# Query and key rows cross DRAM once in float32, and GpSimd splits them per head

## The chip, the cores and the metric

One core of a Trainium2 chip runs the whole kernel. The metric is the device time of one execution in microseconds, the median of several runs. One core has TensorE (matrix products into PSUM), VectorE, ScalarE, GpSimd and SyncE (SP, which here issues all DMAs, in order, on one queue).

## The reference

Two sequences of 1024 tokens (width 1024, float32) go through one encoder layer with shared weights:

- `h = rmsnorm(x)`, then one input projection into q, k, v of mixer A (8 heads x 64) and the compressed c_q (256), c_kv (128), k_rope (32) of mixer B.
- Mixer A: rotary on q and k, then attention with three (window, dilation) patterns merged by their softmax denominators. The kernel computes it as one dense softmax with a table of log counts (`logc`) added to the scores.
- Mixer B: q = rmsnorm(c_q) @ w_uq (64 + 32 rotary columns a head), k and v from rmsnorm(c_kv) @ w_ukv, a rotary key that the heads share, dense softmax.
- Both outputs are normalised, concatenated and projected by w_o, with a residual; then a gated MLP (2816 wide) with a width-3 convolution over positions, residual, final rmsnorm.

## The kernel before, in words

**Precision.** Products are made of float32r matmuls on pairs: each float32 operand is split into a high part (a copy to float32r, on ScalarE) and a low part (the operand less the high part, on VectorE), and a product takes three passes hi*hi, hi*lo, lo*hi. All engines run their own instruction stream; semaphores (`s_...`) tie them together. The work of each engine stands in program order, so an instruction that waits holds up what stands behind it, and so does a DMA issue that waits on SP.

**Stages, for each of the two sequences:**

1. *Query and key products of mixer A* (`qk_unit`, U = 0..3, token half h = 0, 1, so r = 2U + h = 0..7; each U needs two weight tiles w_hi/w_lo, split by `w_hi_split` on ScalarE and `w_lo_split` on VectorE). VectorE rotates the product (`rope`, L1093) into `mc`, ScalarE makes `rq_hi` (`rope_hi`, L806), VectorE `rq_lo` (`rope_lo`, L1106), and SP writes both parts to DRAM (`write_qk`, L259, 8 DMAs for each r). Going through DRAM turns the layout into one of rows per head.
2. *v products* (16, L547 on; `v_hi` L819 on ScalarE, `v_lo` L1124 on VectorE), with weights `vst` loaded by `load_vc` (L268) and split by `vc_hi` (L811) and `vc_lo` (L1111). `load_vc(s, 2)` and `load_vc(s, 3)` bring the two halves of the weight w_c of the next stage. In ScalarE's and VectorE's order their splits stand behind v_hi/v_lo 9 and 11, ahead of 12 to 15.
3. *c products* (8 token tiles), normalised and transposed. The first waits for the whole split of w_c (s_vwl) and for v_lo(12).
4. *Attention A* (`attention`, PE at L564, ScalarE at L880, VectorE at L1212): 64 steps, 8 heads x 8 query tiles. A step G: scores(G+3), row_max and nm on VectorE, exp on ScalarE, transposes of the probabilities, their split pt_hi/pt_lo, and the products with v. scores takes the head's rows in `q2`, `khh`, `kll`, in two buffers, which `load_head_a` (L279, 5 DMAs, 1.5 MB) fills from DRAM for both parts; it waits for the scores of two heads earlier.
5. *Projections of mixer B* (14 units, i = 0..13: 0 and 1 rotary q, then q and k in turn to 9, then v in 10..13), in three PSUM pairs. For i < 10 ScalarE makes `b_hi`, VectorE `b_lo` (three buffers of each), SP writes both to DRAM (`write_b`, L304). Unit i from 5 on waits for b_lo of unit i - 3. The rotary key of all heads is transposed at i = 5 and placed in both heads' buffers (`krh`, `krl`).
6. *Attention B*: the same steps with three score passes; `load_head_b` (L291) brings 8 pieces for a head. Before it ScalarE and VectorE wait until every row of stage 5 has been written.
7. *Output projection, MLP*, with TensorE busy nearly throughout. `wo_split(0)` is hooked into attention B at step 40.

GpSimd only splits the weights of mixer B (uq, ukv) at the start of attention A.

**Memory.** The output of the attentions, `o` (32 KB a partition at R_O), lies where wv_hi/wv_lo, the v weights, were. `qh, ql, kh, kl` lie where `q2, khh, kll` and `logc` are.

**SP's order around the change** (L370 to L409): load_vc(2), write_qk(6), write_qk(7), load_head_a(0), logc, load_vc(3), a wait for the c products, load_head_a(1), the weights of mixer B, the other heads of A; then write_b(0) to write_b(3), the rotary key, load_head_b(0), load_head_b(1), write_b(4) to write_b(9), wost, gout, and the other heads of B.

## Time and profile before

| what | value |
|---|---|
| median of 3 runs | 3044.6 us (3040.99 to 3048.77) |
| the profiled execution | 3046.3 us, of which the span of the trace 3044.5 us |
| TensorE (PE) busy | 2922.4 us, 96% |
| VectorE (DVE) busy | 1788.0 us, 59% |
| ScalarE (ACT) busy | 1228.1 us, 40% |
| GpSimd (POOL) busy | 16.8 us, 1% |
| mean granted clock of TensorE | 0.982 |
| DMA | 227.5 MB, mean 75 GB/s |

The table says that TensorE is the engine to look at, and that VectorE and ScalarE have time to spare on average. An average says nothing of a stage: to judge a change, one looks for the stretches in which TensorE stands, and for what released it. A line number in a row is that of the instruction; L467 (`product`) and L1072 (`sub`) are helpers that many stages use, so their rows are told apart by the tiles named. The number in brackets at the end of a row of the timeline is how long the engine had been idle and which instruction released it.

### The profile page before, as it was taken

To read this page: it belongs to the slowest core of one execution; us is meant where nothing else is said; L and a number is where in the kernel's file an instruction comes from. 1 tells how busy PE (TensorE), PEld (TensorE's weight loads), DVE (VectorE), ACT (ScalarE), POOL (GpSimd) and SP (SyncE) were. 2 spreads that over 40 slices of the span, in tenths; PEclk is the share of its full clock that TensorE was granted. 3 is DMA by queue.
4 is the path that set the end of the run, shared out by engine and by line. 5 is a ranking of instruction groups with operands and counts; after the bars stand their busy time and mean duration, and the time that the engine had idled before them with its cause. 6 is when DMAs were issued, how large, how long until landed. Compare 5 with 4: busy or idle time off the path is not lost.

```text
span 3044.5 us, 39362 instructions
## 1 busy us (share of the span) xinstructions
PE 2922.4 (96%) x16272; PEld 2550.9 (84%) x16272; DVE 1788.0 (59%) x2559; ACT 1228.1 (40%) x1990; POOL 16.8 (1%) x12
## 2 busy tenths in 40 slices
...
GB/s 222 149 61 87 43 170 86 80 45 75 31 56 50 76 56 49 56 49 57 61 191 125 59 77 43 200 72 65 46 70 35 49 56 49 42 49 49 49 49 56
DMA packets 170177, 227.50 MB, mean 75 GB/s; under 512 B 23440, under 2 KB 122640, under 8 KB 169488
## 3 DMA queue, kind: packets, MB, share of 16 engines
...
q14 instruction: 47, 0.39, 0.0%
...
## 4 chain that ended last, share of the span: by engine, by line
PE 89%; DVE 5%; ACT 2%; DMA 2%; issue 1%; SPq 1%; DVEq 0%; ACTq 0%
PE pair L467 71%; PE pair L606 7%; PE pair L582 4%; PE pair L583 4%; PE pair L591 2%; DMA q_nope_rows<-b_lo 1%; DVE at_lo L1072 1%; DMA xs<-in_x_t 1%; PE pair L472 0%; DMA xt<-in_x_seqs 0%; ACT at_hi L947 0%; ACT junk L766 0%; DVE at_lo L1082 0%; DVE b_lo L1072 0%; DVE x L1068 0%
## 5 line engine op out<-in xcount | busy, mean ns | idle before, releaser
L467 PE MATMUL pair<-at_hi,wu_hi 128*128 128x512 f32 x1408 | 549.3, 390 | 5.2 <-DVE at_lo L1072 5.2
L467 PE MATMUL pair<-at_hi,wu_lo 128*128 128x512 f32 x1408 | 549.1, 390 | 0.0
L467 PE MATMUL pair<-at_lo,wu_hi 128*128 128x512 f32 x1408 | 549.1, 390 | 0.0
L1072 DVE TENSOR_TENSOR pt_lo<-pair,pt_hi 128x512 fp32r<-128x512 f32 x512 | 329.9, 686 | 99.4 <-ACT pt_hi L902 99.4
L902 ACT CAST pt_hi<-pair 128x512 fp32r<-128x512 f32 x512 | 275.7, 590 | 162.5 <-PE pair L606 155.0
L1403 DVE TENSOR_TENSOR x<-pair,x 128x1024 f32<-128x1024 f32 x176 | 215.2, 1223 | 181.5 <-PE pair L467 180.9
L467 PEld LDWEIGHTS pair<-at_hi,wu_hi 128*128 128x128 f32 x1408 | 265.2, 188 | 60.7 <-DVE at_lo L1072 5.7
L467 PEld LDWEIGHTS pair<-at_hi,wu_lo 128*128 128x128 f32 x1408 | 265.0, 188 | 55.4
L467 PEld LDWEIGHTS pair<-at_lo,wu_hi 128*128 128x128 f32 x1408 | 265.0, 188 | 54.9
L887 ACT ACTIVATE prob<-pair,nm 128x1024 f32<-128x1024 f32 x256 | 289.4, 1131 | 14.6 <-DVE nm L1225 14.3
L467 PE MATMUL pair<-wd_hi,h_hi 128*128 128x512 f32 x704 | 275.4, 391 | 8.1 <-DVE x L1403 8.1
L582 PE MATMUL pair<-pt_hi,v 128*128 128x256 f32 x1024 | 268.6, 295 | 7.2 <-ACT ot L892 5.9
L467 PE MATMUL pair<-wd_lo,h_hi 128*128 128x512 f32 x704 | 275.0, 391 | 0.0
L467 PE MATMUL pair<-wd_hi,h_lo 128*128 128x512 f32 x704 | 274.9, 390 | 0.0
L606 PE MATMUL pair<-idn,prob 128*128 128x128 f32 x2048 | 268.3, 274 | 2.4 <-DVE pt_lo L1072 2.0
L583 PE MATMUL pair<-pt_lo,v 128*128 128x256 f32 x1024 | 257.6, 284 | 0.0
L1367 DVE SCALAR_TENSOR_TENSOR cv<-pair,cw,cv 128x1023 f32<-128x1023 f32 x42 | 53.9, 1282 | 316.0 <-ACT cv L990 316.0
L606 PEld LDWEIGHTS pair<-idn,prob 128*128 128x128 f32 x2048 | 230.8, 141 | 8.1 <-issue 6.1
L582 PEld LDWEIGHTS pair<-pt_hi,v 128*128 128x128 f32 x1024 | 195.8, 191 | 12.9 <-issue 6.3
L583 PEld LDWEIGHTS pair<-pt_lo,v 128*128 128x128 f32 x1024 | 196.7, 192 | 5.2
L960 ACT CAST wd_hi<-ust 128x1024 fp32r<-128x1024 f32 x44 | 44.3, 1052 | 345.0 <-PE pair L467 336.6
L990 ACT ACTIVATE cv<-pair,cw 128x1024 f32<-128x1024 f32 x42 | 50.7, 1207 | 296.8 <-PE pair L467 296.8
...
## 6 DMA issues: line engine op xcount, KB each, us to landing
ust<-in_w_up SPq DMA_DIRECT2D x88, 512.0 KB, 3.9
ust<-in_w_down SPq DMA_DIRECT2D x44, 512.0 KB, 4.4
wst<-in_w_qk SPq DMA_DIRECT2D x16, 512.0 KB, 4.8
...
xt<-in_x_seqs SPq DMA_DIRECT2D x16, 512.0 KB, 3.6
q<-q_rows SPq DMA_DIRECT2D x16, 512.0 KB, 3.6
...
```

The source lines that it names most:

```text
L467: mm = pe.matmul(dst, lhs, rhs, start=(i == 0), stop=(i == n - 1))
L582: pe.matmul(bank(6)[:, 0:2 * P], v2[:, k, h, :], pt_hi[g % 2][:, k, :], start=(k == 0), stop=False)
L583: mm = pe.matmul(bank(6)[:, 0:2 * P], v2[:, k, h, :], pt_lo[g % 2][:, k, :], start=False, stop=(k == NT - 1))
L591: mm = pe.matmul(bank(7)[:, i * HA:(i + 1) * HA], ot[:, i * P:(i + 1) * P], stk[:], start=True, stop=True)
L606: tr = pe.transpose(bank(4 + hb)[:, k * P:(k + 1) * P], prob[G % 2][:, c:c + P], idn[:])
L887: act.activation(prob[G % 2][:], pair[G % 2][:], ACT.Exp, bias=nm[:, G % 4:G % 4 + 1], scale=scale, accum_out=den[:, h % 2, t:t + 1]).then ...
L902: act.copy(pt_hi[G // 2 % 2][:, 4 * hb:4 * hb + 4, G % 2 * P:(G % 2 + 1) * P], bank(4 + hb).rearrange("p (k n) -> p k n", k=4)).then_inc(s ...
L960: act.copy(dst, ust[slot][:]).then_inc(s_uhi, 1)
L990: act.activation(dst[:], pair[b % 2][:], ACT.Identity, bias=cw[b][:, 3:4], scale=cw[b][:, 1:2]).then_inc(s_ci, 1)
L1072: return dve.tensor_tensor(out_, full, hi.bitcast(F32), ALU.subtract)
L1367: dve.scalar_tensor_tensor(buf[:, 1:S], u[:, 0:S - 1], cw[b][:, 0:1], buf[:, 1:S], ALU.mult, ALU.add).then_inc(s_c0, 1)
L1403: dve.tensor_tensor(x1[:, t, :], pair[2 + t % 2][:], x1[:, t, :], ALU.add).then_inc(s_ya, 1)
```

## The change

Rotated q and k (both mixers) are no longer split before they go to DRAM: one float32 row goes out and comes back. GpSimd then makes the high and low parts for each head, in the same two buffers per head as before (`head` in the gpsimd block, a single raw buffer for each of q and k). In mixer A the raw rows land in unused columns of `o`, so their first load waits for the end of the v products; in mixer B they land in R_REST, so that `wost` is loaded after the last split and its split moves from step 40 to 56. Mixer B's projections are evicted by one ScalarE copy each (`bst`, four buffers). Declarations, semaphore names and casts that only follow from this are left out; "..." marks what is left out.

```diff
--- before.py
+++ after.py
-B_WRITES = (4, 3, 3)
+B_WRITES = (3, 3, 2, 2)
...
-mcb = place("mcb", [P, 2, H], F32, R_X)
 msb = place("msb", [P, 2, H], F32, R_X + 4)
-b_hi = [place(f"b_hi{i}", [P, 2, H], F32R, R_X + 8 + 8 * i) for i in range(3)]
-b_lo = [place(f"b_lo{i}", [P, 2, H], F32R, R_X + 12 + 8 * i) for i in range(3)]
-krh = place("krh", [ROT, S], F32R, R_C + 25)
-krl = place("krl", [ROT, S], F32R, R_X + 60)
+bst = [place(f"bst{i}", [P, 2, H], F32, R_X + 8 + 4 * i) for i in range(4)]
+krt = place("krt", [ROT, S], F32, R_C + 25)
+
+
+qraw_a, kraw_a = o[:, 6:8, WA:D], o[:, 4:6, WA:D]
+qraw_b, kraw_b = place("qraw_b", [P, S], F32, R_REST), place("kraw_b", [P, S], F32, R_REST + 4)
...
     def write_qk(s, r):
         U, h = r // 2, r % 2
         dst, a = (kd if U % 2 == 0 else qd), U // 2
-        sp.wait_ge(s_rlo, 8 * s + r + 1)
-        for hl, src in ((0, rq_hi[r % 2]), (1, rq_lo[r % 2])):
-            for i in range(4):
-                to = dst[4 * a + i, hl].rearrange("(o f) s -> f o s", o=2)[:, :, half(h)]
-                sp.dma_start(to, src[ROT * i:ROT * i + ROT, :, :].bitcast(F32)).then_inc(s_qw[r % 2], 16)
+        sp.wait_ge(s_ro, 8 * s + r + 1)
+        for i in range(4):
+            to = dst[4 * a + i].rearrange("(o f) s -> f o s", o=2)[:, :, half(h)]
+            sp.dma_start(to, rq[r % 2][ROT * i:ROT * i + ROT, :, :]).then_inc(s_qw[r % 2], 16)
...
     def load_head_a(s, h):
-        e, a = h % 2, h // 4
-        if h >= 2:
-            sp.wait_ge(s_sc, 128 * s + 8 * (h - 2) + 8)
+        if h:
+            sp.wait_ge(s_hs, 16 * s + h)
         for i in range(2):
-            sp.wait_ge(s_qw[i], 512 * s + 256 * (a + 1))
-        sp.dma_start(q2[e][:], qd[h].rearrange("l f s -> (l f) s")).then_inc(s_hd[e], 16)
+            sp.wait_ge(s_qw[i], 256 * s + 128 * (h // 4 + 1))
         for j in range(2):
             rows = slice(HA * j, HA * j + HA)
-            sp.dma_start(khh[e][rows, :], kd[h, 0]).then_inc(s_hd[e], 16)
-            sp.dma_start(kll[e][rows, :], kd[h, 1]).then_inc(s_hd[e], 16)
+            sp.dma_start(qraw_a[rows, :, :], qd[h].rearrange("d (a n) -> d a n", a=2)).then_inc(s_hd, 16)
+            sp.dma_start(kraw_a[rows, :, :], kd[h].rearrange("d (a n) -> d a n", a=2)).then_inc(s_hd, 16)
 
     def load_head_b(s, h):
-        e, last = h % 2, 3 + 2 * (h // 2)
-        if h >= 2:
-            sp.wait_ge(s_sc, 128 * s + 64 + 8 * (h - 2) + 8)
-        for m in range(3):
-            sp.wait_ge(s_bwr[m], 32 * (B_WRITES[m] * s + len([i for i in range(last + 1) if i % 3 == m])))
-        for hl, qdst, kdst in ((0, qh, kh), (1, ql, kl)):
-            sp.dma_start(qdst[e][0:HA, :], qnd[hl, h * HA:(h + 1) * HA, :]).then_inc(s_hd[e], 16)
-            for o_ in range(2):
-                sp.dma_start(qdst[e][HA + 16 * o_:HA + 16 * o_ + 16, :],
-                             qrd[hl, o_, 16 * h:16 * h + 16, :]).then_inc(s_hd[e], 16)
-            sp.dma_start(kdst[e][0:HA, :], knd[hl, h * HA:(h + 1) * HA, :]).then_inc(s_hd[e], 16)
+        last = 3 + 2 * (h // 2)
+        if h:
+            sp.wait_ge(s_hs, 16 * s + 8 + h)
+        for m in range(4):
+            sp.wait_ge(s_bwr[m], 16 * (B_WRITES[m] * s + len([i for i in range(last + 1) if i % 4 == m])))
+        rows = slice(h * HA, (h + 1) * HA)
+        sp.dma_start(qraw_b[0:HA, :], qnd[rows, :]).then_inc(s_hd, 16)
+        for o_ in range(2):
+            sp.dma_start(qraw_b[HA + 16 * o_:HA + 16 * o_ + 16, :], qrd[o_, 16 * h:16 * h + 16, :]).then_inc(s_hd, 16)
+        sp.dma_start(kraw_b[0:HA, :], knd[rows, :]).then_inc(s_hd, 16)
 
     def write_b(s, i):
-        sp.wait_ge(s_bl, 14 * s + i + 1)
-        for hl, src in ((0, b_hi[i % 3]), (1, b_lo[i % 3])):
-            if i < 2:
-                to = qrd[hl].rearrange("o p s -> p o s")[:, :, half(i)]
-                sp.dma_start(to, src[:].bitcast(F32)).then_inc(s_bwr[i % 3], 16)
-            else:
-                dst, n = (qnd if i % 2 == 0 else knd), (i - 2) // 2
-                sp.dma_start(dst[hl, n * P:(n + 1) * P, :],
-                             src[:].bitcast(F32).rearrange("p a n -> p (a n)")).then_inc(s_bwr[i % 3], 16)
+        if i < 2:
+            sp.wait_ge(s_bro, 2 * s + i + 1)
+            to = qrd.rearrange("o p s -> p o s")[:, :, half(i)]
+            sp.dma_start(to, bst[i % 4][:]).then_inc(s_bwr[i % 4], 16)
+        else:
+            sp.wait_ge(s_bcp, 8 * s + i - 1)
+            dst, n = (qnd if i % 2 == 0 else knd), (i - 2) // 2
+            sp.dma_start(dst[n * P:(n + 1) * P, :], bst[i % 4][:].rearrange("p a n -> p (a n)")).then_inc(s_bwr[i % 4], 16)
...
+        sp.dma_start(logc[:], log_count).then_inc(s_logc, 16)
+        sp.wait_ge(s_vm, 16 * (s + 1))
         load_head_a(s, 0)
-        sp.wait_ge(s_qw[1], 512 * s + 512)
-        sp.dma_start(logc[:], log_count).then_inc(s_logc, 16)
         load_vc(s, 3)
-        sp.wait_ge(s_cm, NT * (s + 1))
         load_head_a(s, 1)
         sp.wait_ge(s_vwl, 4 * s + 4)
+        sp.wait_ge(s_cm, NT * (s + 1))
         sp.dma_start(uq_st[:], w_uq).then_inc(s_bw, 16)
         sp.dma_start(ukv_st[:], w_ukv).then_inc(s_bw, 16)
 
@@ -393,23 +388,23 @@
 
         for i in range(4):
             write_b(s, i)
-        sp.wait_ge(s_krl, s + 1)
-        for e in range(2):
-            sp.dma_start(kh[e][HA:HB, :], krh[:].bitcast(F32)).then_inc(s_krw, 16)
-            sp.dma_start(kl[e][HA:HB, :], krl[:].bitcast(F32)).then_inc(s_krw, 16)
+        sp.wait_ge(s_bfree, 2 * (s + 1))
         load_head_b(s, 0)
+        write_b(s, 4)
+        sp.wait_ge(s_krh, s + 1)
+        sp.dma_start(kraw_b[HA:HB, :], krt[:]).then_inc(s_krw, 16)
+        for i in range(5, 10):
+            write_b(s, i)
+        sp.dma_start(gout[:], g_out.partition_broadcast(P)).then_inc(s_og, 16)
         load_head_b(s, 1)
-        for i in range(4, 10):
-            write_b(s, i)
-        sp.dma_start(wost[:], w_o_v[:, :, 0:COL]).then_inc(s_wost, 16)
-        sp.dma_start(gout[:], g_out.partition_broadcast(P)).then_inc(s_og, 16)
         sp.wait_ge(s_bm, 14 * s + 14)
-        sp.wait_ge(s_krw, 64 * (s + 1))
         for h in range(2, HEADS):
             load_head_b(s, h)
             for t in range(NT):
                 if t * 6 // NT + 2 == h:
                     sp.dma_start(x1[:, t, :], x_v[s * NT + t]).then_inc(s_x1[t], 16)
+        sp.wait_ge(s_hs, 16 * (s + 1))
+        sp.dma_start(wost[:], w_o_v[:, :, 0:COL]).then_inc(s_wost, 16)
...
             if 3 <= i < 5:
                 pe.wait_ge(s_bfree, 2 * s + i - 2)
-            if i >= 5:
-                pe.wait_ge(s_bl, 14 * s + i - 2)
+            elif 5 <= i < 13:
+                pe.wait_ge(s_bcp, 8 * s + i - 4)
+            elif i == 13:
+                pe.wait_ge(s_bl, 4 * s + 1)
...
                 if t == 0:
-                    pe.wait_ge(s_hd[h % 2], head_landed(h))
+                    pe.wait_ge(s_hs, (2 * s + mixer) * HEADS + h + 1)
...
-        w_hi_split(s, 2)
-        w_hi_split(s, 3)
-        for r in range(3):
-            rope_hi(r)
-        w_hi_split(s, 4)
-        w_hi_split(s, 5)
-        rope_hi(3)
+        for j in range(2, 6):
+            w_hi_split(s, j)
         vc_hi(0)
...
-        for i in range(14):
+        for i in range(2, 14):
+            act.wait_ge(s_bm, 14 * s + i + 1)
             if i < 10:
-                src = mcb[:] if i < 2 else pair[i % 3][:].rearrange("p (a n) -> p a n", a=2)
-                act.wait_ge(s_bro if i < 2 else s_bm, 2 * s + i + 1 if i < 2 else 14 * s + i + 1)
-                free(act, s_bwr[i % 3], 32 * (B_WRITES[i % 3] * s + i // 3))
-                act.copy(b_hi[i % 3][:], src).then_inc(s_bh, 1)
+                free(act, s_bwr[i % 4], 16 * (B_WRITES[i % 4] * s + i // 4))
+                act.copy(bst[i % 4][:], pair[i % 3][:].rearrange("p (a n) -> p a n", a=2)).then_inc(s_bcp, 1)
...
-        for m in range(3):
-            act.wait_ge(s_bwr[m], 32 * B_WRITES[m] * (s + 1))
-        attention(1, SCALE_B, {40: lambda: wo_split(0), 63: lambda: o_stats(0)})
+        for m in range(4):
+            act.wait_ge(s_bwr[m], 16 * B_WRITES[m] * (s + 1))
+        attention(1, SCALE_B, {56: lambda: wo_split(0), 63: lambda: o_stats(0)})
...
         def rope(r):
-            h = r % 2
+            h, q = r % 2, rq[r % 2]
             src = pair[r % 3][:].rearrange("p (o n) -> p o n", o=2)
             dve.wait_ge(s_mq, 16 * s + 2 * r + 2)
-            free(dve, s_rlo, 8 * s + r)
+            free(dve, s_ro, 8 * s + r)
+            free(dve, s_qw[r % 2], 256 * s + 64 * (r // 2))
             if r < 2:
                 dve.wait_ge(s_tabs, 2 * s + r + 1)
-            dve.tensor_tensor(mc[:], src, cost[:, half(h)].unsqueeze(1).to_broadcast([P, 2, H]), ALU.mult).then_inc(s_mc, 1)
+            dve.tensor_tensor(q[:], src, cost[:, half(h)].unsqueeze(1).to_broadcast([P, 2, H]), ALU.mult)
             dve.tensor_tensor(ms[:], src, sint[:, half(h)].unsqueeze(1).to_broadcast([P, 2, H]), ALU.mult).then_inc(s_ms, 1)
             dve.wait_ge(s_ms, 8 * s + r + 1)
-            dve.tensor_tensor(mc[:, 0, :], mc[:, 0, :], ms[:, 1, :], ALU.subtract)
-            dve.tensor_tensor(mc[:, 1, :], mc[:, 1, :], ms[:, 0, :], ALU.add).then_inc(s_ro, 1)
-
-        def rope_lo(r):
-            dve.wait_ge(s_rhi, 8 * s + r + 1)
-            free(dve, s_qw[r % 2], 512 * s + 128 * (r // 2))
-            sub(rq_lo[r % 2][:], mc[:], rq_hi[r % 2][:]).then_inc(s_rlo, 1)
+            dve.tensor_tensor(q[:, 0, :], q[:, 0, :], ms[:, 1, :], ALU.subtract)
+            dve.tensor_tensor(q[:, 1, :], q[:, 1, :], ms[:, 0, :], ALU.add).then_inc(s_ro, 1)
...
-        for i in range(14):
-            src = pair[i % 3][:].rearrange("p (a n) -> p a n", a=2)
-                dve.tensor_tensor(mcb[:], src, cosbt[:, half(i)].unsqueeze(1).to_broadcast([P, 2, H]), ALU.mult)
-                dve.tensor_tensor(msb[:], src, sinbt[:, half(i)].unsqueeze(1).to_broadcast([P, 2, H]), ALU.mult).then_inc(s_bfree, 1)
-                dve.wait_ge(s_bfree, 2 * s + i + 1)
-                dve.tensor_tensor(mcb[:, 0, :], mcb[:, 0, :], msb[:, 1, :], ALU.subtract)
-                dve.tensor_tensor(mcb[:, 1, :], mcb[:, 1, :], msb[:, 0, :], ALU.add).then_inc(s_bro, 1)
...
+        for i in range(2):
+            src, q = pair[i][:].rearrange("p (a n) -> p a n", a=2), bst[i]
+            dve.wait_ge(s_bm, 14 * s + i + 1)
+            free(dve, s_bwr[i], 16 * B_WRITES[i] * s)
+            if i:
+                dve.wait_ge(s_bro, 2 * s + i)
+            dve.tensor_tensor(q[:], src, cosbt[:, half(i)].unsqueeze(1).to_broadcast([P, 2, H]), ALU.mult)
+            dve.tensor_tensor(msb[:], src, sinbt[:, half(i)].unsqueeze(1).to_broadcast([P, 2, H]), ALU.mult).then_inc(s_bfree, 1)
+            dve.wait_ge(s_bfree, 2 * s + i + 1)
+            dve.tensor_tensor(q[:, 0, :], q[:, 0, :], msb[:, 1, :], ALU.subtract)
+            dve.tensor_tensor(q[:, 1, :], q[:, 1, :], msb[:, 0, :], ALU.add).then_inc(s_bro, 1)
+            if i == 0:
+                last_osum()
+        for i in range(10, 14):
+            t = 2 * (i - 10)
+            dve.wait_ge(s_bh, 4 * s + i - 9)
+            sub(v2[:, t:t + 2, :, HA:P], pair[i % 3][:].rearrange("p (t h x) -> p t h x", t=2, x=HA),
+                v2[:, t:t + 2, :, 0:HA]).then_inc(s_bl, 1)
...
     for s in range(N_SEQ):
+        def head(mixer, h, copies, rests):
+            n, e = (2 * s + mixer) * HEADS + h, h % 2
+            pool.wait_ge(s_hd, 64 * (n + 1))
+            if n:
+                pool.wait_ge(s_hs, n)
+            if h >= 2:
+                pool.wait_ge(s_sc, 8 * (n - 1))
+            for to, raw in copies(e):
+                pool.tensor_copy(to, raw).then_inc(s_hh, 1)
+            pool.wait_ge(s_hh, 3 * n + 2)
+            k_rest, q_rest = rests(e)
+            sub(*k_rest).then_inc(s_hh, 1)
+            pool.wait_ge(s_hh, 3 * n + 3)
+            sub(*q_rest).then_inc(s_hs, 1)
+
+        halves = lambda a: a.rearrange("p (a n) -> p a n", a=2)
+        hi_a = lambda e: ((halves(q2[e][:]), qraw_a), (halves(khh[e][:]), kraw_a))
+        lo_a = lambda e: ((halves(kll[e][:]), kraw_a, halves(khh[e][:])),
+                          (halves(q2[e][HA:P, :]), qraw_a[HA:P, :, :], halves(q2[e][HA:P, :])))
+        hi_b = lambda e: ((qh[e][0:HB, :], qraw_b[0:HB, :]), (kh[e][0:HB, :], kraw_b[0:HB, :]))
+        lo_b = lambda e: ((kl[e][0:HB, :], kraw_b[0:HB, :], kh[e][0:HB, :]),
+                          (ql[e][0:HB, :], qraw_b[0:HB, :], qh[e][0:HB, :]))
+
+        head(0, 0, hi_a, lo_a)
+        pool.wait_ge(s_cm, NT * (s + 1))
+        head(0, 1, hi_a, lo_a)
         pool.wait_ge(s_bw, 32 * (s + 1))
+        pool.wait_ge(s_hs, 16 * s + 2)
         pool.tensor_copy(uq_hi[:], uq_st[:]).then_inc(s_bhi, 1)
         pool.tensor_copy(ukv_hi[:], ukv_st[:]).then_inc(s_bhi, 1)
         pool.wait_ge(s_bhi, 2 * s + 1)
-        pool.tensor_tensor(uq_lo[:], uq_st[:], uq_hi[:].bitcast(F32), ALU.subtract).then_inc(s_blo, 1)
+        sub(uq_lo[:], uq_st[:], uq_hi[:]).then_inc(s_blo, 1)
         pool.wait_ge(s_bhi, 2 * s + 2)
-        pool.tensor_tensor(ukv_lo[:], ukv_st[:], ukv_hi[:].bitcast(F32), ALU.subtract).then_inc(s_blo, 1)
+        sub(ukv_lo[:], ukv_st[:], ukv_hi[:]).then_inc(s_blo, 1)
+        pool.wait_ge(s_blo, 2 * s + 2)
+        for h in range(2, HEADS):
+            head(0, h, hi_a, lo_a)
+        pool.wait_ge(s_krw, 16 * (s + 1))
+        pool.wait_ge(s_max, 128 * s + 64)
+        for h in range(HEADS):
+            head(1, h, hi_b, lo_b)
```

## Rows read from the trace of the kernel before

**Rows 1.** The page: busy time of each engine, and the chain that ended last.
```profile
PE 2922.4 (96%) x16272; PEld 2550.9 (84%) x16272; DVE 1788.0 (59%) x2559; ACT 1228.1 (40%) x1990; POOL 16.8 (1%) x12
...
PE 89%; DVE 5%; ACT 2%; DMA 2%; issue 1%; SPq 1%; DVEq 0%; ACTq 0%
```

**Rows 2.** TensorE's waits, whole run: us in total, times, the longest.
```profile
PE pair L467 <- DVE b_lo L1072: 43.5, 8, 19.3
...
PE pair L467 <- DVE w_lo L1072: 9.5, 4, 4.0
```

**Rows 3.** Stretches: length; busy us of PE, PEld, DVE, ACT, POOL; PEclk, DMA share, GB/s.
```profile
202.00:402.00 200.00, 194.84 (x1416) 181.11 (x1416) 180.12 (x393) 155.39 (x298) 8.31 (x4) 0.99 0.25 68
402.00:464.00 62.00, 36.02 (x145) 27.28 (x143) 27.59 (x27) 15.76 (x17) 0.00 (x0) 0.83 0.74 246
464.00:685.00 221.00, 217.19 (x1501) 199.99 (x1502) 173.89 (x316) 155.29 (x294) 0.00 (x0) 0.99 0.24 63
73.30:80.00 6.70, 6.70 (x23) 5.39 (x24) 5.55 (x6) 2.09 (x2) 0.00 (x0) 0.77 0.87 232
449.00:456.00 7.00, 6.91 (x18) 5.34 (x19) 3.96 (x5) 3.95 (x4) 0.00 (x0) 0.55 1.03 420
```

**Rows 4.** Timeline, mixer B's projections of both sequences: start, duration in us.
```profile
401.92 0.40 PE L467 MATMUL pair<-ct_hi,uq_hi 128*128 128x512 f32 x1
402.15 0.40 PE L467 MATMUL pair<-ct_hi,uq_lo 128*128 128x512 f32 x1
...
439.48 0.43 SPq L312 DMA_DIRECT2D q_nope_rows<-b_lo  x1
...
446.77 1.01 ACT L917 CAST b_hi<-pair 128x1024 fp32r<-128x1024 f32 x1 [19.23 <-DMA q_nope_rows<-b_lo]
...
449.10 0.79 PE L467 MATMUL pair<-ukv_hi,ct_hi 128*128 128x512 f32 x1 [18.39 <-DVE b_lo L1072]
...
460.12 0.47 PE L467 MATMUL pair<-kh,qh 96*128 96x512 f32 x1 [2.41 <-issue]
...
1914.78 0.40 PE L467 MATMUL pair<-ct_hi,uq_hi 128*128 128x512 f32 x1
...
1973.31 0.47 PE L467 MATMUL pair<-kh,qh 96*128 96x512 f32 x1 [2.41 <-issue]
```

**Rows 5.** Timeline, query and key products of sequence 0.
```profile
73.30 0.77 PE L467 MATMUL pair<-at_hi,w_hi 128*128 128x512 f32 x1 [3.97 <-DVE w_lo L1072]
...
70.79 1.23 DVE L1072 TENSOR_TENSOR rq_lo<-mc,rq_hi 128x1024 fp32r<-128x1024 f32 x1 [1.11 <-ACT rq_hi L809]
```

**Rows 6.** DMA issues, 398 to 470 us: KB each, median us to landing.
```profile
q_nope_rows<-b_hi SPq DMA_DIRECT2D x4, 512.0 KB, 5.5
```

**Rows 7.** Timeline from v to c products; last row: DMA issues, 202 to 216.
```profile
151.31 0.34 SPq L276 DMA_DIRECT2D vst<-in_w_c  x1
...
155.93 1.58 ACT L817 CAST wc_hi<-vst 128x1664 fp32r<-128x1664 f32 x1 [2.29 <-DMA vst<-in_w_c]
...
159.43 0.87 DVE L1127 SCALAR_TENSOR_TENSOR v<-pair,xrs,v 128x256 fp32r<-128x256 f32 x2
...
164.49 0.35 PE L467 MATMUL pair<-wc_hi,at_hi 128*128 128x416 f32 x1
...
205.11 0.60 SPq L289 DMA_DIRECT2D kll<-k_rows  x1
...
uq_st<-in_w_uq SPq DMA_DIRECT2D x1, 768.0 KB, 8.1
```

**Rows 8.** Groups: GpSimd's of the run; pt_lo of 215.0 to 223.4, of the run.
```profile
L1459 POOL TENSOR_TENSOR ukv_lo<-ukv_st,ukv_hi 128x1024 fp32r<-128x1024 f32 x2 | 4.8, 2404 | 0.0
...
L1455 POOL CAST ukv_hi<-ukv_st 128x1024 fp32r<-128x1024 f32 x2 | 2.1, 1045 | 0.0
...
L1072 DVE TENSOR_TENSOR pt_lo<-pair,pt_hi 128x512 fp32r<-128x512 f32 x6 | 3.8, 682 | 0.0
...
L1072 DVE TENSOR_TENSOR pt_lo<-pair,pt_hi 128x512 fp32r<-128x512 f32 x512 | 329.9, 686 | 99.4 <-ACT pt_hi L902 99.4
```

More of the change, by code:

```diff
@@ L85, in encoder_kernel @@
         sint = place("sint", [P, S], F32, R_Q + 36)
-        mc = place("mc", [P, 2, H], F32, R_Q + 40)
         ms = place("ms", [P, 2, H], F32, R_Q + 44)
-        rq_hi = [place(f"rq_hi{i}", [P, 2, H], F32R, R_Q + 48 + 8 * i) for i in range(2)]
-        rq_lo = [place(f"rq_lo{i}", [P, 2, H], F32R, R_Q + 52 + 8 * i) for i in range(2)]
+        rq = [place(f"rq{i}", [P, 2, H], F32, R_Q + 48 + 4 * i) for i in range(2)]
         wv_hi = [place(f"wv_hi{i}", [P, NK, COL], F32R, R_O + 16 * i) for i in range(2)]
@@ L189, in encoder_kernel @@
         s_logc = sem("log_count_landed")
-        s_hd = [sem(f"head_rows_landed{i}") for i in range(2)]
+        s_hd, s_hh, s_hs = sem("head_rows_landed"), sem("head_rows_hi"), sem("head_rows_split")
         s_sc, s_max, s_nm, s_pr = sem("scores_ready"), sem("row_max"), sem("minus_max_ready"), sem("probs_ready")
@@ L194, in encoder_kernel @@
         s_bw, s_bhi, s_blo, s_tabb = sem("b_weights_landed"), sem("b_weights_hi"), sem("b_weights_lo"), sem("b_tables_landed")
[L195 to L197 removed]
+        s_bm, s_bfree, s_bro, s_bcp = sem("b_product_ready"), sem("b_product_taken"), sem("b_rotated"), sem("b_copied")
+        s_bh, s_bl = sem("b_v_hi"), sem("b_v_lo")
+        s_bwr = [sem(f"b_rows_written{i}") for i in range(4)]
+        s_krt, s_krh, s_krw = sem("k_rope_transposed"), sem("k_rope_copied"), sem("k_rope_placed")
         s_ss, s_std, s_rs, s_xn = sem("squares_summed"), sem("rms_ready"), sem("rrms_ready"), sem("tile_normalised")
@@ L562, in _, with attention @@
                         c_transposed(t - 1)
-                def attention(mixer, score_passes, head_landed, between=None):
+                def attention(mixer, score_passes, between=None):
                     b, bg = (2 * s + mixer) * STEPS, (2 * s + mixer) * GROUPS
@@ L804, in _ @@
                 tb = 2 * NT * s
-                def rope_hi(r):
-                    act.wait_ge(s_ro, 8 * s + r + 1)
-                    free(act, s_qw[r % 2], 512 * s + 128 * (r // 2))
-                    act.copy(rq_hi[r % 2][:], mc[:]).then_inc(s_rhi, 1)
                 def vc_hi(i):
@@ L855, in _ @@
                 vc_hi(1)
-                rope_hi(6)
-                rope_hi(7)
                 for i in range(16):
```

85 lines of the change are left out of this document (26 added, 59 removed).

## The prediction

> **What bounds the kernel now.** I read the page first. TensorE is busy 96% of the span and holds 89% of the chain that ended last [rows 1]. So a part of VectorE's or ScalarE's work that goes is worth nothing by itself; only what TensorE waits for counts. The view of who waited for whom, for TensorE, names two places that this change touches: 43.5 us behind the low halves of mixer B's rows (b_lo), 19.3 us of it at once, and 9.5 us behind w_lo [rows 2]. The table by stage shows where that lies: in the 62 us of mixer B's projections TensorE is busy 36 us at a mean clock of 0.83, while both attentions run near 98% busy [rows 3].
>
> *Mixer B's projections.* The first product starts at 401.92, the first scores of mixer B at 460.12: 58.2 us; in sequence 1, 1914.78 to 1973.31, 58.5 us [rows 4]. ScalarE stands 19.2 us before a b_hi copy because its buffer is still being written out, and TensorE stands 18.4 us behind it [rows 4]. The write it waits for was issued only at 439.48: on SP's queue, in order, both heads' loads (L400, L401) stood ahead of it [rows 4]. After the pause TensorE ran at a clock of 0.55 for 7 us [rows 3], so 0.45 * 7 = 3.2 us of work are lost on top. That is the lower of its two levels (1.2 of 2.4 GHz) for most of the stretch, and what it did before was to stand still.
>
> *Query and key products.* At 73.30 TensorE has waited 3.97 us for w_lo of the third unit. In the code ScalarE splits that weight only behind rope_hi(2), VectorE behind rope_lo(2), which ran at 70.79 [rows 5]. The clock is 0.77 over the next 6.7 us [rows 3]: 1.5 us more.
>
> **The change, part by part.**
>
> (a) Query/key stage. Eight rope_hi and eight rope_lo per sequence go, and half of the write DMAs. ScalarE can split weight 4 when the first half of unit (1, 1) is done, some 5 us before TensorE needs it at 73.3 - 4.0 = 69.3. VectorE reached it after rope_lo(2), at 70.79 + 1.2 = 72.0; each rope_lo cost it 1.23 us and a wait of 1.11 [rows 5], and of the three before this point the first lies in idle time before the second unit's table. So it comes 2 * 2.3 us earlier, at 67.3, and the low half is there at 68.5. Weight 5 can be split from 69.3 on, is done by 71.6, and is wanted half a unit later, 24 matmuls at 0.23 us or 5.5 us after 69.3. The wait goes: 4.0 + 1.5 = 5.5 us per sequence, **11 us**. Bounds: 4 in all if one of the two stays, 11 if both go. I take 11, as both are the same wait (4 waits, longest 4.0, [rows 2]). What is late next there is nothing up to the v products.
>
> (b) Projection stage of B. TensorE's own work is 6 units of 12 matmuls and 8 of 6, at 0.227 us from one start to the next (two starts in [rows 4], 0.23, and the 24 of two units at 5.45 us): 27.3 us, with last_osum and krot's transposes 28.5. The way from the last product to the first scores was 2.4 us [rows 4] and stays (a copy and a subtraction). Now the remaining waits, walked through queue by queue. Unit 4 waits for the second msb product: 0.1. Row buffers: write 3 is issued at about 414 and lands at 418.5 (5.5 us for a q_nope write at its median, [rows 6]; 4.5 for one alone, my choice, since half the bytes are gone); load_head_b(0) waits on SP for exactly that, takes 2.2 us of issue, and holds write 4 behind it until 421, landed 425.5; copy 8 needs that buffer, so unit 11 waits 0.1 and the later copies run 1 us behind; unit 13 waits about 1 us for v_lo(10), the last v_lo ends 1 us later than before. Sum 28.5 + 2.4 + 1.8 = 32.7 us. GpSimd must have head 0 split by then: rows and rotary key landed at about 424, plus 6.9 us (below) is 431, and scores would start at 434.6. So 3.6 us of margin; past them each us costs one. Gain (58.2 - 32.7) + (58.5 - 32.7) = **51 us**. Bounds: no waits left, 30.9 us, gives 55; head 0 late by 7 us, a whole split, gives 37. I take 51, as the walk has the split ahead. ScalarE and VectorE both wait for all writes; the last (copy 9, about 428) lands by 433, before scores(0) is finished.
>
> (c) The second half of w_c. Today load_vc(3) is issued at 151.31 while v products run, the split is done and TensorE goes over to the c products at 164.49 with no idle time [rows 7]. The raw buffers of mixer A lie in o, which is wv_hi/wv_lo of the second half, so load_head_a(0) must now wait for all 16 v products (s_vm), and load_vc(3) stands behind it on SP. ScalarE's vc_hi(3) stands before v_hi(12) and the c products wait for it. So TensorE stands from 164.5 on: four DMA issues at 0.60 and a little each [rows 7], 2.5 us; then the landing. Alone it takes 4.6 us (151.31 to 155.93); the weight load issued behind a whole head of 1.5 MB took 8.1 [rows 7]; behind 1 MB, in proportion, 4.6 + 3.5 * 2/3 = 6.9, which I take. From the landing to the first low half that TensorE needs 155.93 to 159.43 + 0.5 = 4.0. Sum 13.4 us. The clock after it by the row after the 18.4 us pause: 3.2 us, at least the 1.5 seen after the 4 us pause. Together 16.6, twice: **33 us lost**. Bounds per sequence: 2.5 + 4.6 + 4.0 + 1.5 = 12.6 and 2.5 + 8.1 + 4.0 + 3.2 + 2.4 (one GpSimd instruction in VectorE's way) = 20.2.
>
> (d) GpSimd's splits. A copy of 1024 columns by the ukv_hi row 1.04 us, a subtraction by the ukv_lo row 2.40 [rows 8]: 2 * 1.04 + 2 * 2.40 = 6.9 us per head (the half of q2 has as many columns, so no less). A step of attention takes 200/64 = 3.1 us in A and 221/64 = 3.45 in B, a head 25 and 28. Load, 2.5 us of issue, 5 to 6 landing and the split fit twice. Head 1 of A starts on GpSimd when the c products end and is wanted some 20 us later; the weight splits of 8.3 us follow it and head 2 follows them, still about 15 us ahead. Head 1 of B: issued at 431 behind gout, landed 438, split 445, wanted some 24 us after the first scores. Nothing on the path while TensorE sets the pace. Is VectorE slowed by it? While GpSimd made its four weight splits (215.0 to 223.4), pt_lo took 682 ns, over the whole run 686 [rows 8]: no.
>
> (e) wost is loaded after the last split and split at step 56, not 40. GpSimd ends head 7 about two steps after step 45, the load of 1 MB lands some 9 us later, at step 50. The same two instructions, covered by the slack of 221 - 174 us that VectorE has in this stage [rows 3]; without that cover 1.9 us on ScalarE, twice. Cost nothing. Writes and reads of rows fall by half; no stage is bound by them but (b), where it is counted. The rest of the diff (types, names) costs nothing.
>
> **Sum:** -11 - 51 + 33 = -29 us against the profiled execution's own 3046.3 (span 3044.5 and 1.8 around it): 3017. The median of the runs shown is 1.7 us lower, so I say **3016**.
>
> **A rule against it.** VectorE's wc_lo reads two SBUF tiles, and no row of this trace shows such an instruction beside GpSimd. Head 0's rows are issued from 165 on and land some 5 us later; the split would run from about 170 to 177. vc_lo(3) starts at about 175.5 (173.9 and ScalarE's copy, 1.6) and would be blocked 1.4 us if the two exclude each other, a whole subtraction of 2.4 at worst: 3 to 5 us in two sequences, 3020. The Trainium skill ("SBUF — State Buffer", Who interferes with whom) says that a VectorE instruction with two SBUF inputs and a GpSimd one that reads SBUF do exclude each other. By that rule the time would be this rival's; no row of this trace decides it.
>
> **Rivals.**
> 1. The stall of (c) does not appear, or most of it is hidden: 3016 - 33 = 2983. For it: only that TensorE goes over without idle time today. Against: the order on SP's queue. Chance 0.05.
> 2. Head 0 of mixer B comes late: a new wait on s_hs takes the place of b_lo. With a split and landing 10 us past 434.6 in each sequence: 3036 to 3040. For it: margin of only 3.6 us, and write 4 behind the load. Chance 0.08.
> 3. The exclusion of VectorE by GpSimd at the one place above: 3020, inside my range. Chance 0.25; the plain forecast has 0.58.
> 4. Slower: GpSimd slows VectorE through both attentions. It is active 32 * 6.9 = 221 us, half in A, where VectorE is busy 90%, half in B with 79% [rows 3]. A slowing by a share s costs 110 * (0.90(1+s) - 1) + 110 * (0.79(1+s) - 1) us, as only what passes 100% counts: a third costs 28 and eats the gain up, 0.39 costs 38 and is measurably slower, a half costs 59: 3016 + 59 = 3075. Against: 682 to 686 [rows 8]. Chance 0.04.
>
> **Range and chances.** 0.3% (9 us) is about what a measurement of this kernel can tell from no change. Bounds of the terms: best -11 - 55 + 25 = -41 (3004), worst -4 - 37 + 40 = -1 (3044); both ends together are unlikely, so 3036 above, and a little below the best for a clock that holds up, 3000. That leaves out rival 1, rival 4 and half of rival 2. Faster needs less than 3035.5: forecast, rivals 1 and 3 and a part of 2, 0.88. Same: rest of rival 2 and the bad end of the terms, 0.08. Slower 0.04.
>
> **What would show it.** TensorE's wait for b_lo gone, mixer B's scores some 33 us after the first projection; a new wait of 13 us before the first c product, its last link SP's late vst load; no w_lo wait near 70; GpSimd some 240 us busy, 1.04 and 2.40 us a piece; pt_lo still near 686 ns. I am wrong if TensorE waits for GpSimd at a head's start, if vst lands before the v products end, or if attention's steps grow past 3.1 and 3.45 us.

## The result, and the profile after

The changed kernel takes 3036.4 us (median of 14 runs, 3032.8 to 3037.9) where the kernel before takes 3041.6 (14 runs, 3037.9 to 3048.8). The ratio is 0.998, with a 95% interval of 0.9972 to 0.9989: 3 to 9 us faster, inside the 0.3% that the prediction called no change. Forecast were 3016 us, 29 less than before. The profiled spans differ a little more: 3044.5 before, 3035.9 after, so 8.6 us less; the walk through the stages below adds up to this figure, not to the 5 us between the medians.

The page of after, to be read beside [rows 1]: GpSimd goes from 16.8 to 236.6 us, VectorE and ScalarE lose 28 and 21 us of work, and TensorE, which sets the pace, loses 3.

```profile
PE 2919.5 (96%) x16272; PEld 2553.0 (84%) x16272; DVE 1760.2 (58%) x2521; ACT 1206.9 (40%) x1970; POOL 236.6 (8%) x140
```

The view of who waited for whom, TensorE, whole run of after (us in total, times, longest), to be read beside [rows 2]:

```profile
PE pair L462 <- DVE v L1100: 32.7, 2, 16.5
...
PE pair L511 <- DVE ct_lo L1048: 14.8, 2, 7.4
...
PE pair L462 <- DVE v L1048: 5.5, 4, 2.4
...
PE pair L462 <- DVE w_lo L1048: 5.2, 3, 3.6
```

The 43.5 us behind b_lo are gone. In their place stand 32.7 us at the start of the c products, in two waits, which was forecast, and 14.8 us at their end, which was not (1.26 us each before). The wait for w_lo is only halved.

The same in TensorE's milestones, the start of one instruction in each kernel. The last column says how far the changed kernel is behind (+) or ahead (-) at that point; a step between two rows of it is what the stage between them cost or gave.

| milestone | before, seq. 0 | after | ahead/behind | before, seq. 1 | after | ahead/behind |
|---|---|---|---|---|---|---|
| in the first query/key unit | | | | 1553.45 | 1545.15 | -8.3 |
| first c product | 164.49 | 175.23 | +10.7 | 1678.42 | 1686.14 | +7.7 |
| first scores | 203.74 | 216.92 | +13.2 | 1717.63 | 1726.75 | +9.1 |
| third block of scores | 209.62 | 228.93 | +19.3 | 1723.55 | 1738.80 | +15.3 |
| first product of mixer B | 401.92 | 421.87 | +20.0 | 1914.78 | 1931.52 | +16.7 |
| first scores of mixer B | 460.12 | 453.76 | -6.4 | 1973.31 | 1963.29 | -10.0 |

Read down, sequence 0: 10.7 lost by the start of the c products, 2.4 in them, 6.1 at their end, 0.7 in attention A, then 26.3 won in mixer B's projections (58.2 us to 31.9). Sequence 1 wins 26.7 there (58.5 to 31.8).

Mixer B's end of that, in the timeline of after (start, duration; in brackets the idle time before and who ended it): ahead of the first scores stand only the 2.4 us of copy and subtraction that stood there before.

```profile
421.87 0.40 PE L462 MATMUL pair<-ct_hi,uq_hi 128*128 128x512 f32 x1
...
453.76 0.80 PE L462 MATMUL pair<-kh,qh 96*128 96x512 f32 x1 [2.36 <-DVE v L1048]
...
1931.52 0.40 PE L462 MATMUL pair<-ct_hi,uq_hi 128*128 128x512 f32 x1
...
1963.29 0.50 PE L462 MATMUL pair<-kh,qh 96*128 96x512 f32 x1 [2.36 <-DVE v L1048]
```

The start of the c products; the first row is the same pair of subtractions in the kernel before, the others are from the timeline of after:

```profile
157.55 1.96 DVE L1072 TENSOR_TENSOR wc_lo<-vst,wc_hi 128x1248 fp32r<-128x1248 f32 x2 [3.39 <-ACT wc_hi L817]
...
161.38 0.59 SPq L275 DMA_DIRECT2D vst<-in_w_c  x1
...
168.08 1.58 ACT L804 CAST wc_hi<-vst 128x1664 fp32r<-128x1664 f32 x1 [20.33 <-DMA vst<-in_w_c]
...
168.38 2.34 POOL L1411 TENSOR_TENSOR kll<-o,khh 128x1024 fp32r<-128x1024 f32 x1
...
169.69 4.99 DVE L1048 TENSOR_TENSOR wc_lo<-vst,wc_hi 128x1248 fp32r<-128x1248 f32 x2 [21.42 <-ACT wc_hi L804]
...
170.80 3.44 POOL L1411 TENSOR_TENSOR q<-o,q 64x1024 fp32r<-64x1024 f32 x1
...
175.23 0.69 PE L462 MATMUL pair<-wc_hi,at_hi 128*128 128x416 f32 x1 [16.47 <-DVE v L1100]
```

TensorE ends the v products at 158.76; the load of the weight's second half is issued 2.6 us later, behind the four loads of head 0 (2.5 were forecast), and TensorE stands 16.5 us. There is more in this wait than the late load. The row of wc_lo covers two instructions (128x1248 and 128x416); they took 1.96 us before, when nothing of GpSimd ran, and 4.99 beside GpSimd's split of head 0. GpSimd's second subtraction grew too, from 2.4 to 3.44 us. The releaser in the last row is named v and not wc_lo, because v's low part stands behind wc_lo on VectorE.

The end of the c products in the timeline of after: the last token tile's normalisation, and in the last row TensorE, which transposes the result only behind it. The first row is that transposition in the kernel before:

```profile
207.09 0.52 PE L519 MATMUL pair<-idn,cr 128*128 128x128 f32 x3 [1.26 <-DVE ct_lo L1072]
...
213.54 0.49 DVE L1166 SCALAR_TENSOR_TENSOR cr<-cr,rs,glora 128x256 f32<-128x256 f32 x1
...
216.19 1.04 POOL L1422 CAST q<-o 128x1024 fp32r<-128x1024 f32 x1 [41.95 <-PE pair L462]
...
218.29 2.36 POOL L1411 TENSOR_TENSOR kll<-o,khh 128x1024 fp32r<-128x1024 f32 x1
218.41 2.52 DVE L1166 SCALAR_TENSOR_TENSOR cr<-cr,rs,glora 128x256 f32<-128x256 f32 x1
220.73 2.40 POOL L1411 TENSOR_TENSOR q<-o,q 64x1024 fp32r<-64x1024 f32 x1
220.85 2.42 DVE L1167 SCALAR_TENSOR_TENSOR cr<-cr,rs,glora 128x128 f32<-128x128 f32 x1
223.26 1.46 POOL L1442 CAST uq_hi<-uq_st 128x1536 fp32r<-128x1536 f32 x1
223.31 1.45 DVE L1170 TENSOR_TENSOR prb<-cr,sinb 128x16 f32<-128x16 f32 x1
...
226.40 0.87 PE L511 MATMUL pair<-idn,cr 128*128 128x128 f32 x3 [7.40 <-DVE ct_lo L1048]
```

Head 1's split starts on GpSimd on the last c product's semaphore (s_cm). VectorE's normalisation of the last c tile starts from the same event. The tile before it, at 213.54 with GpSimd idle, takes 0.49 us. The last tile's takes 2.52, its second part, of half the columns, 2.42, and even a 128x16 product 1.45: each ends within 0.3 us of the GpSimd instruction beside it, whatever its own size. Readers should look at that pattern, instructions of VectorE that end when GpSimd's do, rather than at busy shares: both engines are far from full here.

The query and key stage of sequence 1, where only 0.2 us of the predicted 5.5 came:

```profile
1552.58 5.86 SPq L356 DMA_DIRECT2D out_y<-x  x8
1558.48 11.90 SPq L265 DMA_DIRECT2D k_rows<-rq  x8
...
1572.23 1.23 DVE L1077 TENSOR_TENSOR rq<-pair,cost 128x1024 f32<-128x1024 f32 x1 [4.39 <-DMA k_rows<-rq]
...
1577.20 0.76 PE L462 MATMUL pair<-at_hi,w_hi 128*128 128x512 f32 x1 [3.58 <-DVE w_lo L1048]
```

VectorE's rotation writes straight into the float32 buffer that is written out, so rope(r) now begins with a wait for the write of rope(r - 2). In sequence 1 the row writes stand on SP behind eight writes of the previous output, VectorE waits 4.39 us for its buffer, the subtraction for w_lo stands behind it, and TensorE waits 3.58 us for w_lo, where the kernel before waited 3.98 at this place.

### The profile page after: what moved, and what is told of

Its sections match the earlier page's. It is cut to its first block and busy times, and to the rows that moved or that the text cites. A ratio compares the mean times of both kernels' runs of the same rounds, so it can differ in the third digit from the quotient of the medians.

```text
span 3035.9 us, 39278 instructions
## 1 busy us (share of the span) xinstructions
PE 2919.5 (96%) x16272; PEld 2553.0 (84%) x16272; DVE 1760.2 (58%) x2521; ACT 1206.9 (40%) x1970; POOL 236.6 (8%) x140
## 5 line engine op out<-in xcount | busy, mean ns | idle before, releaser
L574 PEld LDWEIGHTS pair<-pt_hi,v 128*128 128x128 f32 x1024 | 194.8, 190 | 12.9 <-issue 6.3
```

What stands on the lines that cost most here:

```text
L574: pe.matmul(bank(6)[:, 0:2 * P], v2[:, k, h, :], pt_hi[g % 2][:, k, :], start=(k == 0), stop=False)
```

## The experiments

Theory: two things took the gain. **First**, the second half of w_c is loaded late, as predicted. **Second**, VectorE instructions with their inputs in SBUF and GpSimd's split shut each other out, at two places on the path, the c weight and the last c tile. The rivals: GpSimd's split is harmless and TensorE waits for something else at those places; or what is taken away at one place comes back as another wait. Times of the kernel before, taken beside the experiments, were 3043.4 for the first four (9 runs) and 3042.7 for the others (15 runs), where it was 3041.6 beside the change. The ratios below are against those. The change itself was not measured again, so a difference from its 3036.4 us can be off by some 2 us for that, on top of the spread of the 4 to 8 runs of each experiment.

**1. The late load alone.** In the order on SP:

```diff
+                load_vc(s, 3)
                 sp.wait_ge(s_vm, 16 * (s + 1))
                 load_head_a(s, 0)
-                load_vc(s, 3)
```

> Second half of w_c loaded before the wait for the v products, rest as in the changed kernel (3036.4 us). Theory (SP's order makes the stall ahead of the c products): the 16.5 and 16.3 us waits go and with them some 2 us of low clock each, minus 37 us, but GpSimd's split of head 0 now falls on the normalisations of the c tiles, which can cost up to 5 us per sequence: 2999 to 3010 us. Rival (TensorE would have waited anyway, for the weights or for v_lo): over 3030 us, with a wait over 8 us left ahead of the c products.

Measured: 3005.9 us, ratio 0.9879 (0.9866 to 0.9893), 30.5 us faster than the change as it was. The stall ahead of the c products is gone from the list of waits, the one for ct_lo is as it was, and a small new one appears, for krot. TensorE's waits of this kernel:

```profile
PE pair L511 <- DVE ct_lo L1048: 14.8, 2, 7.4
...
PE pair L511 <- DVE krot L1173: 5.5, 2, 2.8
```

The new one is the exclusion again, moved: wc_lo is now past, and head 0's split falls on the first c tiles. The subtraction that makes krot, 0.19 us alone, takes 2.22, and then the next tile's normalisation 2.59. From the timeline of this kernel:

```profile
168.89 2.34 POOL L1411 TENSOR_TENSOR kll<-o,khh 128x1024 fp32r<-128x1024 f32 x1
169.06 2.22 DVE L1173 TENSOR_TENSOR krot<-pra,prb 128x32 f32<-128x32 f32 x1
...
171.31 2.39 POOL L1411 TENSOR_TENSOR q<-o,q 64x1024 fp32r<-64x1024 f32 x1
171.39 2.59 DVE L1166 SCALAR_TENSOR_TENSOR cr<-cr,rs,glora 128x256 f32<-128x256 f32 x1
```

So the wait for all v products belongs to the loads of the heads (their raw rows lie in the memory of wv_hi and wv_lo), not to the w_c load that stood behind them. It was the order of two calls that cost 30 us. That is a net figure: with the late load went the exclusion at the c weight (6 us, experiment 3), and the 5.5 us of krot came.

**2. Head 1's split behind the normalisations.**

```diff
                 pool.wait_ge(s_cm, NT * (s + 1))
+                pool.wait_ge(s_cn, NT * (s + 1))
                 head(0, 1, hi_a, lo_a)
```

> GpSimd starts head 1's split only when the last c tile is normalised and rotated; nothing else changes. Theory (the two SBUF inputs of VectorE's normalisation are shut out while GpSimd reads): the 7.4 us waits before the last c transposes fall to the 1.3 us of the kernel before, the low clock after them goes in part, minus 12 to 15 us: 3021 to 3025 us; the two normalising instructions take 0.48 and 0.34 us again. Rival (the wait comes from something else that is late, the table load on ScalarE or TensorE itself): no change, 3036 us.

Measured: 3021.1 us, ratio 0.9932 (0.992 to 0.9945), 15 us faster than the change. Among VectorE's groups (us busy in all, mean ns) the normalisation is back at its old 485 ns; the first row is the change's, the second this kernel's:

```profile
L1166 DVE SCALAR_TENSOR_TENSOR cr<-cr,rs,glora 128x256 f32<-128x256 f32 x16 | 11.8, 739 | 0.6
```

```profile
L1166 DVE SCALAR_TENSOR_TENSOR cr<-cr,rs,glora 128x256 f32<-128x256 f32 x16 | 7.8, 485 | 0.6
```

The two waits of 7.4 us are back at 1.3. Head 1 is wanted later, and TensorE's list of waits shows none for GpSimd. The five runs spread over 10 us (3016.8 to 3026.8), so the 15 us are good to some 4.

**3. Head 0's split behind the c weight.** The same kind of wait, `pool.wait_ge(s_vwl, 4 * (s + 1))`, ahead of `head(0, 0, hi_a, lo_a)`.

> GpSimd starts head 0's split only when both low parts of w_c's second half are made. Theory (exclusion): wc_lo's two instructions take 1.96 us together again, not 4.99 and 4.82, and the wait ahead of the c products falls from 16.5 to about 13.5 us; but the split now falls on the first normalisations of c, which wait in their turn: minus 6 us less up to 8 us, 3030 to 3038 us. Rival (wc_lo is slow for another reason, as the reads of tiles that a DMA has just written): it keeps its 4.9 us.

Measured: 3030.5 us, ratio 0.9962 (0.9949 to 0.9976), 5.9 us faster than the change. From its timeline, and from its waits of TensorE:

```profile
171.52 1.96 DVE L1048 TENSOR_TENSOR wc_lo<-vst,wc_hi 128x1248 fp32r<-128x1248 f32 x2 [21.54 <-ACT wc_hi L804]
```

```profile
PE pair L462 <- DVE v L1100: 26.8, 2, 13.6
```

The two subtractions are back at 1.96 us, and TensorE's wait falls from 16.5 to 13.6. That splits the stall: 13.6 for the late load (13.4 were forecast) and 3 for the exclusion, 6 in both sequences (rival 3 gave it 3 to 5 in both). One worry of the expectation did not come true: the delayed split ended at 180.5, before the first normalisation at 183.4.

**4. A third buffer for the rotated rows.** rq gets a third buffer in memory that lies free, and its semaphores go by r % 3; two of the places that change are shown.

```diff
-        rq = [place(f"rq{i}", [P, 2, H], F32, R_Q + 48 + 4 * i) for i in range(2)]
+        rq = [place(f"rq{i}", [P, 2, H], F32, R_Q + (48, 52, 40)[i]) for i in range(3)]
...
-                    free(dve, s_qw[r % 2], 256 * s + 64 * (r // 2))
+                    free(dve, s_qw[r % 3], 64 * (QK_WRITES[r % 3] * s + r // 3))
```

> A third buffer for the rotated rows. Theory (in the second sequence VectorE's third rotation waits 4.4 us for the row writes that stand behind eight output DMAs, and w_lo and TensorE behind it): the 3.6 us wait for w_lo in sequence 1 goes, with the low clock after it minus 5 us: 3031 us, sequence 0 as before. Rival (w_lo is late for its own load): wait and time stay, 3036 us.

Measured: 3029.6 us, ratio 0.9956 (0.9944 to 0.9969), 6.8 us faster than the change. The 3.58 us wait is gone; of w_lo's 5.2 us, 1.6 are left in two waits, the longest 0.9. The time fell by more than the wait; the clock after it was expected to give part of that back. What failed in the query and key stage was the buffer's wait and nothing in the splits.

**5. All three of 1, 2 and 4 together.**

> The three edits together: w_c's second half loaded first, head 1's split after the last normalisation, a third buffer for the rotated rows. If the three losses are separate their gains add up: from 3036.4 us minus 30.5 minus 15.3 minus 6.8 is 2984 us. Rival (they overlap: one wait hides another): 2995 us or more.

Measured: 2988.1 us, ratio 0.9826 (0.9812 to 0.9839). Against the change the three alone gave 30.5, 15.3 and 6.8, in sum 52.6; together 48.3. They add up but for 4 us, which is within what these differences are good for, so these were in the main separate causes. The 5.5 us wait for krot of experiment 1 stays.

**6. The same, with head 0's subtractions stepped between the c tiles' normalisations.** Each of the two waits for its tile:

```diff
+                    if gates:
+                        pool.wait_ge(s_cn, gates[0])
                     sub(*k_rest).then_inc(s_hh, 1)
                     pool.wait_ge(s_hh, 3 * n + 3)
+                    if gates:
+                        pool.wait_ge(s_cn, gates[1])
...
-                head(0, 0, hi_a, lo_a)
+                head(0, 0, hi_a, lo_a, (NT * s + 1, NT * s + 2))
```

> As all_three, and in head 0's split GpSimd waits before its first subtraction for the first c tile to be rotated, before the second for the second tile, so that each falls into a pause of VectorE. Theory (exclusion, instruction by instruction): the 2.8 us wait of TensorE for krot in each sequence goes, 2.6 us or so of the normalising instructions that waited too: minus 5 to 8 us against all_three, 2976 to 2979 us. Rival (the wait is ScalarE's chain of squares): no change against all_three.

Measured: 2981.4 us, ratio 0.9803 (0.979 to 0.9817): 61 us below the kernel before and 55 below the change, the best version here. TensorE's wait for krot falls from 5.5 to 1.5 us:

```profile
PE pair L512 <- DVE ct_lo L1049: 2.5, 2, 1.3
...
PE pair L512 <- DVE krot L1174: 1.5, 2, 0.8
```

The gain over experiment 5 is 6.7 us, of which the list of waits accounts for 4. Every run here (2980.1 to 2984.2) is below every run there (2985.0 to 2990.5), but with four and five runs the size of the gain is uncertain. It stops short of what was expected, 2976 to 2979: GpSimd's first cast still collides, and so does its first subtraction, which waits for the first tile only and runs into the second one's normalisation. From its timeline:

```profile
166.50 1.04 POOL L1423 CAST q<-o 128x1024 fp32r<-128x1024 f32 x1 [166.06 <-DMA o<-k_rows]
...
166.50 1.18 DVE L1168 SCALAR_TENSOR_TENSOR cr<-cr,rs,glora 128x128 f32<-128x128 f32 x1
...
169.17 2.39 POOL L1412 TENSOR_TENSOR kll<-o,khh 128x1024 fp32r<-128x1024 f32 x1 [0.59 <-DVE krot L1174]
...
170.53 1.32 DVE L1167 SCALAR_TENSOR_TENSOR cr<-cr,rs,glora 128x256 f32<-128x256 f32 x1
```

**7. Fewer SBUF inputs.** The normalisation multiplies by the row's scale alone, one SBUF tensor in place of two; the gains are left out, so the outputs are not those of the layer. The first of the two lines that change:

```diff
-                    dve.scalar_tensor_tensor(c[:, 0:RQ], c[:, 0:RQ], rs[:, q0:q0 + 1], glora[:, 0:RQ], ALU.mult, ALU.mult)
+                    dve.tensor_scalar(c[:, 0:RQ], c[:, 0:RQ], rs[:, q0:q0 + 1], None, ALU.mult)
```

> The changed kernel with c_q and c_kv scaled by one over their rms alone, by an instruction with a single SBUF input; the gains g_q_lora and g_kv_lora are left out. Theory (the second SBUF input is what GpSimd shuts out): these two instructions take under 0.5 us beside GpSimd's subtractions, the four rotary products after them still wait: the wait before the last c transpose falls from 7.4 us to 3 to 6. Rival (any VectorE read of SBUF is shut out, or one in a faster mode with both ports): one of the two takes over 2 us and the wait stays near 7.4.

Measured: 3036.3 us, ratio 0.9982 (0.9972 to 0.9993): nothing gained. From its timeline:

```profile
212.02 0.35 DVE L1166 TENSOR_SCALAR cr<-cr,rs 128x256 f32<-128x256 f32 x1
...
216.77 2.36 POOL L1411 TENSOR_TENSOR kll<-o,khh 128x1024 fp32r<-128x1024 f32 x1
216.89 2.39 DVE L1166 TENSOR_SCALAR cr<-cr,rs 128x256 f32<-128x256 f32 x1
219.20 2.43 DVE L1167 TENSOR_SCALAR cr<-cr,rs 128x128 f32<-128x128 f32 x1
```

With one SBUF tensor it takes 0.35 us alone and 2.39 beside GpSimd: shut out like the other, and TensorE's wait before the last c transpose stays at 7.3 us. So two SBUF inputs are not needed, and the rival of the expectation came. It had two halves. "Any VectorE read of SBUF is shut out" is refuted by after's own timeline: nm, made by the same operation from one column in SBUF, takes 0.15 us in the middle of a GpSimd subtraction, and never more than 0.156 in 256 times.

```profile
225.71 3.43 POOL L1411 TENSOR_TENSOR uq_lo<-uq_st,uq_hi 128x1536 fp32r<-128x1536 f32 x1
...
227.49 0.15 DVE L1190 TENSOR_SCALAR nm<-mx 128x1 f32<-128x1 f32 x1
```

The other half, a faster mode with both ports, fits the normalisation: this form is faster alone, 0.35 against 0.49 us. No run isolates it, so it is not shown. pt_lo reads one tile of PSUM and one of SBUF and is not slowed.

**8. The gain without the change.** In the kernel before, only head 1's loads are moved on SP behind the writes of mixer B's rows:

```diff
                 load_head_b(s, 0)
-                load_head_b(s, 1)
                 for i in range(4, 10):
                     write_b(s, i)
+                load_head_b(s, 1)
```

> The kernel before, with only the load of mixer B's head 1 moved behind the writes of its rows on SP's queue. Theory (the 18.4 us wait in mixer B's projections is the queue's order): the write that ScalarE waits for goes out 4.4 us earlier and its transfer has 0.77 MB less ahead of it: wait down to 12 to 14 us in each sequence, minus 9 to 14 us against the kernel before. Rival (the bytes of rows in flight, not the order, set the wait): it stays above 17 us and the time within 0.15%.

Measured: 3031.0 us, ratio 0.9965 (0.9952 to 0.9977), 11.7 us faster than the kernel before. TensorE's wait, and from the timeline the write that the copy waits for (issued at 439.48 in [rows 4]) and the copy:

```profile
PE pair L467 <- DVE b_lo L1072: 30.6, 8, 12.5
```

```profile
435.85 0.43 SPq L312 DMA_DIRECT2D q_nope_rows<-b_lo  x1
...
441.62 1.01 ACT L917 CAST b_hi<-pair 128x1024 fp32r<-128x1024 f32 x1 [13.27 <-DMA q_nope_rows<-b_lo]
```

One head's loads ahead of the writes cost 43.5 - 30.6 = 12.9 us of waiting in both sequences (18.4 to 12.5 us in the first, 19.3 to 12.3 in the second). Some 12.4 us per sequence stay. Head 0's load, which waits for both parts of the rows, still stands ahead of the writes; that this is the reason was not tested. So this one move in the old kernel brings at least as much as the whole change did (the two intervals barely overlap), though less than a quarter of the 53 us that the change wins in mixer B.

## Why the prediction failed

**(b), mixer B's projections, was right.** 53.0 us were won (26.3 and 26.7), 51 forecast; the stages took 31.9 and 31.8 us where the walk through the queues gave 32.7; of its 1.8 us of small waits one of 0.5 came, ahead of a v unit at 449.75. Rival 2 did not come: head 0's split ran from 445.3 to 452.3, and the scores waited for their usual 2.4 us. Its margin, though, was 1.5 us and not 3.6: counted from the stage's first product, the split was ready after 30.4 us (29 in the walk), and the scores started 0.8 us sooner than in it.

**(c), the late half of w_c, was right in its mechanism and nearly in its size.** Forecast were 13.4 us of wait and 3.2 of clock, 33 in two sequences. The load alone cost 13.6 (experiment 3, 26.8 in both sequences), with the clock 30.6, and moving it gave 30.5 us (experiment 1). That these two agree is partly chance, since experiment 1 also lost the 6 us of exclusion at the c weight and gained 5.5 for krot. The clock took 2.4 and 1.4 us over the c products, not 3.2: TensorE had stood still 16 us and then ran its first 7 us at a mean granted clock of 0.62 (0.78 in sequence 1), between its two levels and above the 0.55 of [rows 3]. In the table by stage of after (as [rows 3]):

```profile
175.00:182.00 7.00, 6.77 (x23) 6.55 (x24) 1.26 (x4) 0.00 (x0) 0.00 (x0) 0.62 0.65 150
```

**The step that failed is in (d): "Nothing on the path while TensorE sets the pace."** Head 1 of A was placed "on GpSimd when the c products end" and judged only by when its result is wanted. What runs beside it on VectorE was not asked. There the last c tile's normalisation lies on the path, and it was shut out for 6.1 us per sequence, 12.2 in both; taking it away gave 15 (experiment 2), which is within its uncertainty of 12. The exclusion itself was in the prediction, by the section "A rule against it" and rival 3, but only at one place, vc_lo(3), where it cost 3.0 us per sequence, 6 against the 3 to 5 of its price; it should have been walked along every split. Rival 3's condition held, and one place was missing from its price, which was the dearer one. The argument against rival 4 was sound as far as it went (686 ns for pt_lo in both kernels, and attention A only 0.7 and 1.5 us longer), but pt_lo takes one input from PSUM, and it spoke only for instructions of its kind.

The Trainium skill ("SBUF — State Buffer", Who interferes with whom) says that VectorE with two SBUF inputs and GpSimd reading SBUF exclude each other. This trace agrees: 0.49 against 2.52 us and 1.96 against 4.99. One SBUF input was no protection to the normalisation, 0.35 against 2.39 us (experiment 7), but nm, with one such input too, kept its 0.15 us.

**(a), the query and key stage, was over-sized.** Forecast 11 us, won 6. In sequence 0 the c products start 10.7 us late behind a wait of 16.5, so 5.7 were won before it; in sequence 1 the changed kernel falls from 8.3 ahead to 7.7 behind, 16.0, against a wait of 16.2, so 0.2. "The wait goes" looked at what stands before w_lo on ScalarE and VectorE, but a rope_lo less is not all: rope(r) took over the wait for the written buffer, and in sequence 1 that write is behind eight others on SP. The bound of 4 for one wait that stays was the nearer. Experiment 4 took the buffer's wait away and gave 6.8 us.

**The sum again**, by measured steps, against the spans: -6 (a), -53 (b), +30.5 for the late load (waits of 32.7, less 6 for the exclusion in them, and 3.8 of clock), +6 for the exclusion at the c weight, +12 for it at the last c tile, and some 1.5 spread over the other stages. That gives -9; the spans differ by 8.6. Against the forecast of -29, the exclusion put in 18 us and (a) 5, the 1.5 came besides, and (b) and (c) were 4.5 better than forecast.
